# Two borrowed gather slots for the expert stage of a two-block transformer kernel

## The reference, cut to what matters

```python
def peer_ffn(h, q_w, sub_keys, u_tab, v_tab):      # 8 heads, 128 x 128 = 16384 experts
    q = (t @ q_w).reshape(n, PEER_H, 2, PEER_DQ // 2)
    s = jnp.einsum('thpd,hpnd->thpn', q, sub_keys)
    s1, i1 = lax.top_k(s[:, :, 0], 16)
    s2, i2 = lax.top_k(s[:, :, 1], 16)
    ...                                            # the best 16 of the 16 x 16 sums
    gates = jax.nn.softmax(top_s, axis=-1)
    act = jax.nn.gelu(jnp.einsum('chkd,cd->chk', u_tab[i_c], x_c))
    return jnp.einsum('chk,chkd->cd', g_c * act, v_tab[i_c])
```

## Time and profile before

| | |
|---|---|
| median of three runs | 3675.85 us |
| profiled execution, its own time | 3676.11 us |
| its span in the profile | 3674.3 us |
| PE busy | 83% of the span |
| VectorE busy | 65% |
| POOL busy | 16% |
| the gathers' queue | 36864 packets, 268.45 MB |
| all DMA | 854.19 MB, mean 232 GB/s |

### The profile page before, as it was taken

How to read it: one execution, slowest core, us unless ns; L and a number is a source line. 1 busy time by engine, 2 the same in 40 slices (tenths; PEclk the granted TensorE clock), 3 DMA queues, 4 the chain that set the end, 5 groups by cost and what they waited for, 6 DMA issues and landing times. The chain is left out here.

```text
span 3674.3 us, 52170 instructions
## 1 busy us (share of the span) xinstructions
PE 3066.0 (83%) x21162; PEld 2559.3 (70%) x21162; DVE 2384.8 (65%) x4291; ACT 1260.9 (34%) x2037; POOL 586.1 (16%) x321
## 2 busy tenths in 40 slices
PE   7977765666655599888999988999997999997899
PEld 4856652222211299778989886998986898987798
DVE  3677747888888777365768726777726775544554
ACT  1043211111111233354343445344345334343643
POOL 1010024444445300400000050000040000031000
PEclk9988776777767799979999987999998999996999
DMA  8932229999999886414858531867652764542153
GB/s 337 392 123 94 99 88 380 379 366 378 381 390 385 335 321 246 180 47 168 324 184 345 222 139 47 349 231 304 260 188 73 292 252 173 186 182 91 47 195 126
DMA packets 123103, 854.19 MB, mean 232 GB/s; under 512 B 17300, under 2 KB 18580, under 8 KB 21012
## 3 DMA queue, kind: packets, MB, share of 16 engines
q1 hardware_dynamic: 85748, 582.69, 41.4%
q0 software_dynamic: 36864, 268.45, 18.3%
q10 hardware_dynamic: 288, 0.26, 0.0%
HBM read 850.24 MB, written 1.11 MB: 232 GB/s over the span
## 5 line engine op out<-in xcount | busy, mean ns | idle before, releaser
L268 PE MATMUL ps<-h_hi,w_hi 128*128 128x256 f32 x3328 | 956.5, 287 | 53.0 <-DVE h_lo L459 25.9
L193 DVE TENSOR_TENSOR w_lo<-w_ring,w_hi 128x2048 fp32r<-128x2048 f32 x284 | 650.0, 2290 | 473.6 <-ACT w_hi L188 471.7
L269 PE MATMUL ps<-h_lo,w_hi 128*128 128x256 f32 x3328 | 951.9, 286 | 0.0
L270 PE MATMUL ps<-h_hi,w_lo 128*128 128x256 f32 x3328 | 951.6, 286 | 0.0
L188 ACT ACTIVATE w_hi<-w_ring 128x2048 fp32r<-128x2048 f32 x330 | 629.6, 1913 | 658.1 <-PE ps L270 640.9
L268 PEld LDWEIGHTS ps<-h_hi,w_hi 128*128 128x128 f32 x3328 | 645.0, 194 | 63.4 <-DVE h_lo L459 28.9
L269 PEld LDWEIGHTS ps<-h_lo,w_hi 128*128 128x128 f32 x3328 | 645.4, 194 | 3.2
L270 PEld LDWEIGHTS ps<-h_hi,w_lo 128*128 128x128 f32 x3328 | 644.8, 194 | 0.0
L2909 PE MATMUL ps<-expert_rows,expert_diag 128*128 128x512 f32 x512 | 382.4, 891 | 283.7 <-ACT expert_diag L2947 283.7
L193 POOL TENSOR_TENSOR w_lo<-w_ring,w_hi 128x2048 fp32r<-128x2048 f32 x46 | 212.3, 4633 | 2192.2 <-ACT w_hi L188 2192.2
L2909 PEld LDWEIGHTS ps<-expert_rows,expert_diag 128*128 128x128 f32 x512 | 121.1, 260 | 540.5 <-ACT expert_diag L2947 437.9
(11 more groups left out here) (454 smaller groups left out, 3980.4 us busy)
## 6 DMA issues: line engine op xcount, KB each, us to landing
w_ring<-in_w_stream SPq DMA_DIRECT2D x376, 1024.0 KB, 4.8
a_ring<-in_a_stream SPq DMA_DIRECT2D x108, 1024.0 KB, 7.2
a_ring<-in_t_stream SPq DMA_DIRECT2D x36, 1024.0 KB, 10.0
a_ring<-in_m_stream SPq DMA_DIRECT2D x8, 1024.0 KB, 7.3
alibi<-in_alibi SPq DMA_DIRECT2D x3, 2048.0 KB, 8.5
cond_row<-in_cond_row SPq DMA_DIRECT2D x8, 512.0 KB, 3.9
expert_rows<-in_experts,expert_idx POOLq DMA_INDIRECT x256, 9.2
gates<-mod_rows SPq DMA_DIRECT2D x3, 1024.0 KB, 5.8
```

The lines of the kernel that those rows point to most:

```text
L193: pool.tensor_tensor(self.w_halves(n)[1], self.w_item(n), self.w_halves(n)[0], ALU.subtract).then_inc(self.lo_made, 1)
L268: pe.matmul(out, stationary[0], moving[0], start=start, stop=False)
L269: pe.matmul(out, stationary[0], moving[1], start=False, stop=False)
L270: return pe.matmul(out, stationary[1], moving[0], start=False, stop=stop)
```

## The change

The gathers get ten slots in place of eight. Slots 0 to 7 are in `expert_rows` as before; slot 8 is the first two rows of `m.rows`, slot 9 the first two rows of `core.gates`. The rings of gelu results, weights and diagonals become five batches deep. Even gathers still go to VectorE and odd ones to PE; the counts that are waited for are written by `rows_of_dve` and `rows_of_pe`.

Since a slot overwrites `core.gates`, its load leaves `rw_chain_stage`, and `mixed_stage` waits for one load. The gates are now loaded at the end of the expert stage by SyncE, behind the six weight items and behind two waits for the last releases of VectorE and PE. It counts on `gates_in`, so readers of the gates in the second block now wait for it. Before this, SyncE waits for each of ten slots.

```diff
 rw_chain_stage
-            sp.dma_start(core.gates[:].rearrange("p v n -> p (v n)"),
-                         every[:, in_rest * P:].partition_broadcast(P)).then_inc(rows_in.sem, 16)
 mixed_stage
-            dve.wait_ge(rows_in.sem, rows_in.at(32))
+            dve.wait_ge(rows_in.sem, rows_in.at(16))
 constants
-G_SLOTS = 8
+OWN_SLOTS = 8
+G_SLOTS = OWN_SLOTS + 2
+DVE_EVERY = 2
+def rows_of_dve(n):
+    return -(-n // DVE_EVERY)
+def rows_of_pe(n):
+    return n - rows_of_dve(n)
 peer_stage
-        diag = core.sb(ctx, "expert_diag", [P, G_BATCHES, P])
+        diag = core.sb(ctx, "expert_diag", [P, G_BATCHES, PER_BATCH, P])
+        def rows(slot):
+            if slot < OWN_SLOTS:
+                return own_rows[:, slot, :]
+            lent = m.rows if slot == OWN_SLOTS else core.gates
+            return lent[:, 0:2, :].rearrange("p v n -> p (v n)")
 sync
             for slot in range(G_SLOTS):
-                sp.wait_ge(landed[slot].sem, landed[slot].at(16 * EXPERTS // G_SLOTS))
+                sp.wait_ge(landed[slot].sem, landed[slot].at(16 * uses(slot)))
             core.issue_w(sp, W_SLOTS)
+            sp.wait_ge(dve_freed.sem, dve_freed.at(rows_of_dve(EXPERTS)))
+            sp.wait_ge(pe_freed.sem, pe_freed.at(rows_of_pe(EXPERTS)))
+            gates_at = core.mod_rows.rearrange("(a c) p -> a (c p)", a=1)[:, 4 * D:]
+            sp.dma_start(core.gates[:].rearrange("p v n -> p (v n)"),
+                         gates_at.partition_broadcast(P)).then_inc(core.gates_in.sem, 16)
 gpsimd
-                    used = (n - G_SLOTS) // PER_BATCH + 1
-                    by = pe_freed if slot % PER_BATCH else dve_freed
-                    pool.wait_ge(by.sem, by.at(used))
+                    before = n - G_SLOTS
+                    if before % DVE_EVERY:
+                        pool.wait_ge(pe_freed.sem, pe_freed.at(rows_of_pe(before + 1)))
+                    else:
+                        pool.wait_ge(dve_freed.sem, dve_freed.at(rows_of_dve(before + 1)))
 scalar
-                    act.wait_ge(pe_freed.sem, pe_freed.at(b - G_BATCHES + 1))
+                    act.wait_ge(pe_freed.sem, pe_freed.at(rows_of_pe(PER_BATCH * (b - G_BATCHES + 1))))
 after the stage
+    core.gates_in.passed(16)
```

More of the change, by code:

```diff
@@ L2778, in _ @@
                     last.then_inc(turned.sem, 1)
-    rows_in.passed(32)
+    rows_in.passed(16)
     mean.passed(1)
@@ L2848, in tile_of, with uses @@
             return n % UNIT // PEER_TOP
+        def rows(slot):
[3 more added lines that the diff above has]
+            return lent[:, 0:2, :].rearrange("p v n -> p (v n)")
+        def uses(slot):
+            return len(range(slot, EXPERTS, G_SLOTS))
         @block.sync
@@ L2866, in _ @@
                 if n >= G_SLOTS:
-                    used = (n - G_SLOTS) // PER_BATCH + 1
-                    by = pe_freed if slot % PER_BATCH else dve_freed
-                    pool.wait_ge(by.sem, by.at(used))
+                    before = n - G_SLOTS
[3 more added lines that the diff above has]
+                        pool.wait_ge(dve_freed.sem, dve_freed.at(rows_of_dve(before + 1)))
                 at = n % UNIT
-                pool.indirect_dma_start(rows[:, slot, :], None, core.io["experts"],
+                pool.indirect_dma_start(rows(slot), None, core.io["experts"],
                                         bass.IndirectOffsetOnAxis(ap=idx[:, n // UNIT, at:at + 1], axis=0)).then_inc(
@@ L2904, in _ @@
             for b in range(BATCHES):
[L2905 to L2913, removed]
+                for n in range(PER_BATCH * b, PER_BATCH * (b + 1)):
+                    if n % DVE_EVERY == 0:
+                        continue
+                    t = tile_of(n)
+                    pe.wait_ge(diagonal.sem, diagonal.at(rows_of_pe(n + 1)))
+                    for half in range(2):
+                        last = pe.matmul(core.y[:, 2 * t + half, :], diag[:, b % G_BATCHES, n % PER_BATCH, :],
+                                         rows(n % G_SLOTS)[:, D + half * BANK:D + (half + 1) * BANK],
+                                         start=t not in opened,
+                                         stop=n // UNIT == PEER_H - 1 and n % PEER_TOP == PEER_TOP - 1)
+                    opened.add(t)
+                    last.then_inc(pe_freed.sem, 1)
                 if b in HEADS_LATER:
@@ L2945, in _ @@
                 if b >= G_BATCHES:
-                    act.wait_ge(pe_freed.sem, pe_freed.at(b - G_BATCHES + 1))
-                act.activation(diag[:, b % G_BATCHES, :], core.ident[:], ACT.Copy,
-                               scale=coef[:, b % G_BATCHES, 1:2]).then_inc(diagonal.sem, 1)
+                    act.wait_ge(pe_freed.sem, pe_freed.at(rows_of_pe(PER_BATCH * (b - G_BATCHES + 1))))
+                for e in range(PER_BATCH):
+                    if (PER_BATCH * b + e) % DVE_EVERY:
+                        act.activation(diag[:, b % G_BATCHES, e, :], core.ident[:], ACT.Copy,
+                                       scale=coef[:, b % G_BATCHES, e:e + 1]).then_inc(diagonal.sem, 1)
                 if b in HEADS_LATER:
@@ L3041, in products @@
                     dve.wait_ge(landed[slot].sem, landed[slot].at(16 * (n // G_SLOTS + 1)))
-                    last = dve.tensor_tensor_reduce(rows[:, slot, 0:D], rows[:, slot, 0:D], core.h2[:, tile_of(n), :], 1.0,
+                    u = rows(slot)[:, 0:D]
+                    last = dve.tensor_tensor_reduce(u, u, core.h2[:, tile_of(n), :], 1.0,
                                                     0.0, ALU.mult, ALU.add, dot[:, b % G_BATCHES, e:e + 1])
@@ L3051, in sums @@
                 dve.tensor_tensor(c, c, gates[:, n // UNIT, at:at + PER_BATCH], ALU.mult).then_inc(weighed.sem, 1)
+                if n % DVE_EVERY:
+                    return
                 dve.wait_ge(weighed.sem, weighed.at(b + 1))
-                if b:
-                    dve.wait_ge(dve_freed.sem, dve_freed.at(b))
+                if n:
+                    dve.wait_ge(dve_freed.sem, dve_freed.at(rows_of_dve(n)))
                 t = tile_of(n)
-                dve.scalar_tensor_tensor(out=acc[:, t, :], in0=rows[:, n % G_SLOTS, D:2 * D], scalar=c[:, 0:1],
+                dve.scalar_tensor_tensor(out=acc[:, t, :], in0=rows(n % G_SLOTS)[:, D:2 * D], scalar=c[:, 0:1],
                                          in1=acc[:, t, :], op0=ALU.mult, op1=ALU.add).then_inc(dve_freed.sem, 1)
             def finish(t, batches):
-                dve.wait_ge(pe_freed.sem, pe_freed.at(batches))
-                dve.wait_ge(dve_freed.sem, dve_freed.at(batches))
+                dve.wait_ge(pe_freed.sem, pe_freed.at(rows_of_pe(PER_BATCH * batches)))
+                dve.wait_ge(dve_freed.sem, dve_freed.at(rows_of_dve(PER_BATCH * batches)))
                 for half in range(2):
@@ L3094, in peer_stage @@
     listed.passed(PEER_H)
-    for s in landed:
-        s.passed(16 * EXPERTS // G_SLOTS)
-    for s in (dots, acts, weighed, diagonal, dve_freed, pe_freed):
+    for slot, s in enumerate(landed):
+        s.passed(16 * len(range(slot, EXPERTS, G_SLOTS)))
+    core.gates_in.passed(16)
+    for s in (dots, acts, weighed):
         s.passed(BATCHES)
+    dve_freed.passed(rows_of_dve(EXPERTS))
+    for s in (diagonal, pe_freed):
+        s.passed(rows_of_pe(EXPERTS))
 class Modulation:
```

2 lines of the change are left out of this document (1 added, 1 removed).

## The result

| | median, us | runs | lowest and highest | profiled execution: time, span |
|---|---|---|---|---|
| before | 3676.97 | 6 | 3671.13 to 3684.18 | 3676.11, 3674.3 |
| after | 3645.28 | 6 | 3638.03 to 3652.64 | 3645.80, 3644.0 |

The ratio is 0.9916, with a 95% interval of 0.9903 to 0.9930: 31.7 us less by the medians, 30.3 less by the two profiled spans. In the experiments further down, the time behind "against" is the median of the kernel before, run again beside that group of kernels, and the brackets hold the 95% interval of the ratio.

The account below looks back on a forecast made before the run. The expert stage was taken as bound alternately by VectorE's choice bursts, with DMA idle for want of slots, and by DMA throughput. Seven phases at 4.97 us gave 34.8, other edits 0: 3676.1 - 34.8 = 3641.3, said as 3641, range 3628 to 3658.

Parts of the forecast that it names:

- What bounds the stage: Expert stage: choice phases bound by VectorE, DMA losing 8.3 us each for want of slots; batches behind bound by DMA throughput.
- Seven phases at 4.97 us: Expert stage: two more slots land later gathers two places earlier, 4.97 us gained per choice phase, 34.8 us in all.
- rival (b): Five score-pass units: PE's late slot moves with the deeper ring, only the last two phases gain, 9.9 us, 3666; chance 0.10.
- The choice phases as they were: Expert stage: choice phases still take some 48 us each, VectorE and PE being unchanged up to the late slot.
- DMA near 390 GB/s in the choice: Choice phases of the expert stage: sign of being right, DMA rate rising from 349 to near 390 GB/s.
- Row waits of about 70: Expert stage: sign of being right, VectorE's waits for gathered rows fall from 103 to about 70 us.
- The other edits at nothing: Changed wait counts, five-deep rings and the gates' load moved to the expert stage's end: together 0 us.
- the cover: Behind the expert stage: idle DMA hides the moved gates' load; uncovered, it would cost 3.7 to 12.2 us.
- (a): Rival, five units with score passes: slots short at a second place, 8 us more, 3633; stage floor 631 us; chance 0.09.
- (c): Rival, expert stage: the two extra gathers are issued but don't run ahead, time stays 3676; chance 0.05.
- (d): Rival: expert stage already at the DMA's floor, as by a fixed rate limit below 422 GB/s; 3676; chance 0.02.
- (e): Rival, expert stage: gathers run slower the more are in flight; at 380 GB/s 69 us more, 3710; chance 0.04.

Follow-up runs that it names:

- second profiles: The unchanged kernel and the ten-slot kernel each run and profiled once more: 3676.97 us against 3679.95 (ratio 0.9994), and 3646.88 against 3680.37 (0.9904).
- PE kept busy: Ten-slot kernel plus three extra, overwritten 128 x 512 matmuls in each score pass's batch and the two before: 3640.53 us against 3679.95, ratio 0.9895.

## Why the prediction was right, and where it was not

**What bounds the stage: right.** Bursts of VectorE work with the DMA idle for want of slots, then a DMA-bound stretch at 4.98 us a batch. Nine, ten and twelve slots take the idle time away step by step, and with twelve the share is 1.01 over the seven units.

**Seven phases at 4.97 us: right.** Predicted 34.8 us in the stretches behind the choice, measured 34.1 (to 36.4 with the second profiles), single ones between 4.08 and 6.06. The five units with a score pass gain like the two others, 4.08 to 5.86 against 4.85 and 6.06: rival (b) falls. The short batches are there; in the unit shown, 3.68 three times and 4.79, not four below 3.8.

**The choice phases as they were: wrong by 6.7 us.** The prediction said some 48 us; after has 51.03, 49.55, 51.35, 49.76 in four units with a score pass, and 47.08 and 47.09 in the two without. Before had 48.10, 50.21, 48.47 and 48.10 in those four. The term was set to zero because VectorE and PE were taken to be unchanged up to the late slot. The wait for the gelu, 6.4 us in before, was never priced: it depends on PE's clock level at the start of a score pass. Therefore the stage gave 27.6 us (30.2 at most with the second profiles) and not 34.8. Chance behind the stage gave 3.6 back in the profiles; by the medians the kernel gained 31.7. That the forecast of 3641 lies only 4 us off is in part owed to that.

**DMA near 390 GB/s in the choice: half right.** It was 371 in the phase with the late pass and 422 in a phase without a score pass. The rate is low only because the phase is long: 371 x 51.0 is 18.9 MB, and 349 x 48.1 was 16.8, so two gathers more came in, as forecast. Row waits of about 70: 71.7.

**The other edits at nothing: right.** Ratio 1.0002 without the slots. The gates' load (KB, us from issue to landing in the first line, of the DMA issues) landed at 1232.6 + 17.4 = 1250.0. That is 22.7 us after the first weight issue at 1227.31, where 18.7 were worked out; the cover was wide enough for that, since the DMA then moved nothing for ten microseconds (second line, a window):

```profile
gates<-mod_rows SPq DMA_DIRECT2D x1, 1536.0 KB, 17.4
```

```profile
1250.00:1260.00 10.00, 7.35 (x55) 6.40 (x54) 8.04 (x16) 7.86 (x15) 0.00 (x0) 1.00 0.00 0
```

**The rivals.** (a), that more would go than the slots' own transfer time, did not come about with the ten slots of after, whose rest stretches lost 4.9 a phase. With PE kept busy as well they lost 37.3 in all, 2.5 more than 34.8, so a little of (a) is there once no pass is late. The floor that (a) named, 631 us for the stage, fits the runs: twelve slots come within 5 us of it. (c) falls: the time from issue to landing grew from 9.2 to 11.8 us at an unchanged batch, so more gathers are on their way. By that count it is five in place of four, and not the six that the prediction took for ten slots; twelve slots put six on their way. (d), a floor from a fixed rate below the 422 GB/s, falls with 418 GB/s over 559 us. The Trainium skill, "SBUF — State Buffer", Summary: rules for kernel authors, gives about 358 GB/s for such an estimate; the runs here disagree with it for one core. (e) falls: a steady batch takes 4.98 us with eight, ten and twelve slots.

## What to carry to other kernels

Where compute comes in bursts and a transfer is the bound between them, one more buffer is worth its transfer time once per burst, and the sum of all such buffers is capped by the idle time of the transfer engine. Flattening the burst draws on the same idle time: the two add up while some of it is left (20.5 and some 28 us gave 45.0), and not once it is used up (with twelve slots, nothing more). Look at what stands behind a waiting copy on an in-order engine, but ask first whether the path does not run through the thing that it waits for: removing the wait at the reader gave 13 to 14 us and took as much back. A wait in a queue that must reach a barrier is paid by all engines, even where what it issues is not yet needed.

## What was not expected of the hardware

Three extra matmuls in each of three batches kept PE at 2.4 GHz (a granted clock of 1.00) into all five score passes. Without them ScalarE waited 8.98 us for the pass or up to 11.95, from one execution of the same program to the next. One core's gathers held 422 GB/s in undisturbed stretches with eight slots and 418 over 559 us with twelve; more of them in flight did not raise or lower the rate at which a steady batch arrives.
